# Tile 1's U dots in two halves of 64 tokens, half of its scatter under the dots, and a layer's end without its residual add and norm on VectorE

## What is computed

```
h = h + mixer(rmsnorm(h))             # layer 1: pooling; layer 0: attention and mLSTM
xn = rmsnorm(h, norm_ffn_g[layer])
expert, gate = product_key_top16(xn)  # 8 heads x 16 experts per token, of 16384
act = gelu(einsum('tkd,td->tk', u[expert], xn))
h = h + einsum('tk,tkd->td', gate * act, v[expert])

# pooling mixer of layer 1, hn = rmsnorm(h, norm_mix_g[1])
pooled = win_sum(hn) / count - hn     # windows 2/4/8/16 on four channel groups
h = h + einsum('sgc,gcd->sgd', pooled, pool_w) * layer_scale
```

## Time and profile before

| what | value |
|---|---|
| runs | 3057.61, 3053.96, 3052.4 us |
| median | 3053.96 us |
| profiled execution, its own time | 3056.03 us |
| its span | 3054.1 us |
| granted TensorE clock, mean | 0.864 |
| PE busy | 75% of the span |
| DVE busy | 71% |
| ACT busy | 22% |
| POOL busy | 37% |
| moved by DMA | 1059.10 MB, mean 347 GB/s |

### The profile page before, as it was taken

The page is one execution under the profiler, slowest core; times in us unless marked ns, Lnnn a source line. Parts: engine busy times, 40 slices in busy tenths (PEclk is TensorE's granted clock), DMA queues, the critical chain, the costliest instruction groups (busy, mean ns, idle before and its releaser), DMA issues.

```text
span 3054.1 us, 26189 instructions
## 1 busy us (share of the span) xinstructions
PE 2301.6 (75%) x9248; PEld 1683.1 (55%) x9248; DVE 2173.0 (71%) x3243; ACT 679.0 (22%) x1651; POOL 1136.6 (37%) x1028
## 2 busy tenths in 40 slices
PE   8999999688853410999999887888444019999996
PEld 4686555578753300666666556787433007666664
DVE  1342122899999999866666758999999988566667
ACT  1242120112229920300000011222399002000000
POOL 0000000423343333346666614333433333566664
PEclk9999999899985555999999988999755559999998
DMA  5333324899999999699999959999999996999998
GB/s 211 138 114 139 118 108 198 353 419 421 417 374 422 422 421 421 202 410 410 409 409 409 407 201 414 413 421 407 390 421 422 421 411 214 410 409 409 409 409 338
DMA packets 194530, 1059.10 MB, mean 347 GB/s; under 512 B 21856, under 2 KB 22240, under 8 KB 121312
## 3 DMA queue, kind: packets, MB, share of 16 engines
q0 software_dynamic: 147456, 805.37, 65.2%
q1 hardware_dynamic: 46944, 252.06, 20.8%
HBM read 1055.24 MB, written 2.10 MB: 346 GB/s over the span
## 4 chain that ended last, share of the span: by engine, by line
DMA 46%; PE 23%; DVE 23%; issue 3%; POOL 3%; ACT 1%; DVEq 0%; SPq 0%; ACTq 0%; POOLq 0%
DMA arena<-pu,idx_all 22%; DMA xnT<-pvg,idx_all 14%; DVE arena L1157 11%; DMA arena<-pvg,idx_all 10%; PE bank L1317 7%; DVE h L1183 3%; PE bank L1402 3%; PE bank L1623 2%; PE bank L1557 2%; PE bank L1631 2%; POOL xnT L470 1%; POOL arena L470 1%; PE low L1522 1%; PE bank L1591 1%; PE low L1511 1%
## 5 line engine op out<-in xcount | busy, mean ns | idle before, releaser
L1157 DVE CUSTOM_DVE_ANT_0 arena<-arena,low 128x2048 f32<-128x2048 f32 x420 | 952.6, 2286 | 71.7 <-DMA arena<-pu,idx_all 70.2
L455 POOL DMA_INDIRECT arena<-pu,idx_all x456 | 464.1, 1018 | 1358.8 <-DVE cst L1157 697.1
L1640 PE MATMUL low<-arena 128*128 128x512 f32 x2048 | 904.8, 601 | 9.4 <-DMA arena<-pvd 8.7
L1640 PEld LDWEIGHTS low<-arena 128*128 128x128 f32 x2048 | 597.2, 296 | 316.9 <-DMA arena<-pvd 71.8
L1183 DVE SCALAR_TENSOR_TENSOR h<-arena,cst,h 128x1024 f32<-128x1024 f32 x240 | 307.9, 1286 | 162.9 <-DMA arena<-pvg,idx_all 160.0
L1183 DVE SCALAR_TENSOR_TENSOR h<-xnT,cst,h 128x1024 f32<-128x1024 f32 x240 | 307.6, 1285 | 159.6 <-DMA xnT<-pvg,idx_all 157.1
L470 POOL DMA_INDIRECT arena<-pvg,idx_all x256 | 309.7, 1210 | 244.6 <-DVE h L1183 147.8
L470 POOL DMA_INDIRECT xnT<-pvg,idx_all x256 | 307.7, 1202 | 224.7 <-DVE h L1183 138.4
L1623 PE MATMUL bank<-arena 128*128 128x128 f32 x512 | 132.9, 441 | 201.6 <-ACT arena L747 201.6
L505 ACT ACTIVATE arena<-h 128x2048 f32<-128x2048 f32 (+1 forms) x10 | 17.4, 1740 | 1038.0 <-DVE h L1215 920.2
L1557 PE MATMUL bank<-xnT,arena 128*128 128x256 f32 (+1 forms) x1280 | 235.6, 347 | 11.1 <-issue 5.8
(11 more groups left out here) (233 smaller groups left out, 2203.2 us busy)
## 6 DMA issues: line engine op xcount, KB each, us to landing
arena<-pvd SPq DMA_DIRECT2D x256, 512.0 KB, 6.8
arena<-w_proj SPq DMA_DIRECT2D x22, 2048.0 KB, 7.6
arena<-wq SPq DMA_DIRECT2D x16, 2048.0 KB, 12.5
arena<-w_out SPq DMA_DIRECT2D x9, 2048.0 KB, 7.7
arena<-pu,idx_all POOLq DMA_INDIRECT x494, 14.8
gB<-gains SPq DMA_DIRECT2D x5, 1024.0 KB, 10.4
xnT<-pvg,idx_all POOLq DMA_INDIRECT x256, 14.0
arena<-pvg,idx_all POOLq DMA_INDIRECT x256, 13.9
```

The source lines that it names most:

```text
L455: nc.gpsimd.indirect_dma_start(U[t][slot], None, pu[L], bass.IndirectOffsetOnAxis(row(n), 0)).then_inc(u_got[t][slot], 16)
L1157: vec.tensor_tensor_reduce(out=u, in0=u, in1=low[:, :] if staged else xns[t], scale=1.0, scalar=0.0, op0=ALU.mult, op1=ALU.add, accum_out= ...
L1640: ins = mm(psum[2 * t + c][:, 0:VH], W[t][:, :, n], vdense[:, n % DR, c * VH:(c + 1) * VH], start=n == 0, stop=n == NK - 1)
```

## The change

It has four parts.

1. Tile 1's dots run in two halves of 64 tokens. A column of a half holds two expert slots: partitions 0 to 63 one, 64 to 127 the other, for the same 64 tokens. Indices and gates are rearranged to this layout by four small DMAs each. `duplicate` puts the half's tokens twice into PSUM with four matmuls by a selection matrix; the first dot of a half waits for it. The second half has a ring of six buffers, the last of which is the token tile itself.
2. The first half's weights are made after the 77th dot of tile 1 (index 76), and its 16 quads by ScalarE under the rest of the dots. VectorE makes the 16 quads of the second half after the last dot. `ND`, the number of diagonals, goes from 16 to 8. Two DMAs a half bring the weights back to the layout of the V adds.
3. `h` enters the dense sums by four matmuls with the identity; ScalarE copies the sums to `h` and squares them. The norm ahead of the pooling mixer is dropped: the rows of `PM` are scaled in place by VectorE, the gain is applied where the pooled banks leave PSUM. `pool_w` is loaded in two pieces, and `gain(2)` is not loaded.
4. Dense loads are paced by another rule.

```diff
-UT0, UT1, UP = 6, 7, 3
+UT0, UT1, UT2, UP = 6, 7, 6, 3
...
-LAST_T0 = 16
-ND, DG = 16, 2
+LAST_T0 = 8
+ND, DG = 8, 2
...
+HP = P // 2
+HQ = QUADS // 2
+NSEL = 2 * P + HP + 2
...
-        U = [ring(0, UT0), ring(W_AT + P * P, 2) + [fifth] + ring(0, 4)]
+        U = [ring(0, UT0), ring(W_AT + P * P, 2) + [fifth] + ring(0, 4), [fifth] + ring(0, 4) + [xn1]]
...
+        def pace(n):
+            return (NV - 3) * (n - 2) // NK - (NK - n) // 4
         def landed(m, ring):
...
             def load_vd(L, n):
-                if n > 8:
-                    sp.wait_ge(s["vacc_done"], L * NV + (NV - 8) * (n - 3) // NK)
+                if pace(n) > 0:
+                    sp.wait_ge(s["vacc_done"], L * NV + pace(n))
...
+                idx1 = idx_all[:, PH:2 * PH].rearrange("p g k -> p (g k)")
+                gates1 = gates[:, PH:2 * PH].rearrange("p g k -> p (g k)")
+                sp.dma_start(sel_all, selection).then_inc(s["ld_sel"], 16)
+                sp.wait_ge(s["idx_ready"], ROUTES * (L + 1))
+                for hf in range(2):
+                    for pp, pc, op, oc in quadrants(hf):
+                        sp.dma_start(idx_p[pp, pc], idx1[op, oc]).then_inc(s["ld_idx"], 16)
+                sp.wait_ge(s["gates_ready"], L + 1)
+                for hf in range(2):
+                    for pp, pc, op, oc in quadrants(hf):
+                        sp.dma_start(gates_p[pp, pc], gates1[op, oc]).then_inc(s["ld_gates"], 16)
+                def unfold(hf):
+                    sp.wait_ge(s["w_ready"], 3 * L + hf + 2)
+                    for b in range(2):
+                        sp.dma_start(wv[hf * HP:(hf + 1) * HP, 1, b * HP:(b + 1) * HP],
+                                     w_p[b * HP:(b + 1) * HP, hf, b * HP:(b + 1) * HP]).then_inc(s["ld_wv"], 16)
+                unfold(0)
                 for n in range(NK):
                     load_vd(L, n)
+                    if n == DR - 1:
+                        unfold(1)
...
-                        gain(2 + 2 * L)
+                        gain(3 + L)
                 if L == 0:
...
+                    sp.dma_start(gT, pool_gain).then_inc(s["ld_pm"], 16)
...
-                    sp.dma_start(poolw, pool_w.rearrange("p (g k c) -> p g k c", g=4, k=4)).then_inc(s["ld_pool"], 16)
+                    sp.dma_start(poolw[:, 0].rearrange("p k c -> p (k c)"), pool_w[:, 0:D]).then_inc(s["ld_pool0"], 16)
...
+                    sp.dma_start(poolw[:, 1:4].rearrange("p g k c -> p (g k c)"), pool_w[:, D:4 * D]).then_inc(s["ld_pool1"], 16)
...
-                    gain(3)
...
+                if t and d >= HP:
+                    d -= HP
+                    base = L * NDOT + ND0
+                    if d >= UT2:
+                        pool.wait_ge(s["dot_done"], base + HP + d - UT2 + 1)
+                    elif d == UT2 - 1:
+                        pool.wait_ge(s["dup_ready"], 2 * L + 2)
+                    else:
+                        pool.wait_ge(s["dot_done"], base + max(i for i in range(HP) if i % UT1 == d + 2) + 1)
+                    nc.gpsimd.indirect_dma_start(
+                        U[2][d % UT2], None, pu[L], bass.IndirectOffsetOnAxis(idx_p[:, HP + d:HP + d + 1], 0)
+                    ).then_inc(u_got[2][d % UT2], 16)
+                    return
...
+                    pool.wait_ge(s["ld_idx"], 64 * (L + 1))
...
-                    U[t][slot], None, pu[L], bass.IndirectOffsetOnAxis(row(n), 0)).then_inc(u_got[t][slot], 16)
+                    U[t][slot], None, pu[L], bass.IndirectOffsetOnAxis(idx_p[:, d:d + 1] if t else row(n), 0)
+                ).then_inc(u_got[t][slot], 16)
             def gather_v(L, m):
...
+                e.wait_ge(s["vacc_done"], NV * (o // 2) - LAST_T0 * (1 - t))
+                activation(xns[0][:, t * VG:(t + 1) * VG], h[:, t, VD:D], ACT.Square, accum_out=ss[:, t:t + 1]).then_inc(s["sq_done"], 1)
+            def add_dense(o, t):
+                e.wait_ge(s["dense_done"], o // 2)
+                for c in range(2):
+                    activation(h[:, t, c * VH:(c + 1) * VH], psum[2 * t + c][:, 0:VH], ACT.Copy).then_inc(s["acc_evac"], 1)
+                e.wait_ge(s["acc_evac"], NO * (o // 2 - 1) + 2 * t + 2)
...
+            def gelu(L):
+                e.wait_ge(s["dot_done"], L * NDOT + ND0)
+                e.wait_ge(s["picked"], (L + 1) * NUX)
+                activation(wv[:, 0], act[:, 0], ACT.Gelu).then_inc(s["gelu_done"], 1)
+            def gelu_half(L, hf):
+                e.wait_ge(s["dot_done"], L * NDOT + ND0 + (hf + 1) * HP)
+                cols = act[:, 1, hf * HP:(hf + 1) * HP]
+                activation(cols, cols, ACT.Gelu).then_inc(s["gelu_done"], 1)
...
+                e.wait_ge(s["st_mm"], 3 * L + hf + 2)
+                if hf == 0:
+                    activation(sT[:, 0:2], psum[6][:, 0:2 * P].rearrange("p (a b) -> p a b", a=2), ACT.Copy)
+                activation(sT[:, 2, hf * HP:(hf + 1) * HP], psum[6][:, 2 * P:2 * P + HP], ACT.Copy).then_inc(s["st_ready"], 1)
+            def one_hots(L, n):
+                b, q = n % 2, n % QUADS
...
             for L in range(LAYERS):
                 if L:
+                    e.wait_ge(s["ld_pm"], 32)
...
+                gelu(L)
+                turned(L)
...
-                gelu(L, 1)
-                turned(L, 1)
-                for q in range(QUADS):
-                    if q % (QUADS // ND) == 0:
-                        diagonal(L, q // (QUADS // ND))
-                    spread_out(L, 1, q)
-                norm(2 + 2 * L, 0)
-                square_dense(2 + 2 * L)
-                norm(2 + 2 * L, 1)
+                gelu_half(L, 0)
+                turned_half(L, 0)
+                for q in range(HQ):
+                    one_hots(L, QUADS + q)
+                    if q:
+                        spread_out(L, 1, q - 1)
+                spread_out(L, 1, HQ - 1)
+                gelu_half(L, 1)
+                turned_half(L, 1)
+                for q in range(HQ):
+                    if q % (HQ // ND) == 0:
+                        diagonal(L, q // (HQ // ND))
+                    spread_out(L, 1, HQ + q)
+                o = 2 + 2 * L
+                activation(root_load[:, 1 + L:2 + L], one, ACT.Sqrt)
+                add_dense(o, 0)
+                square_gathered(o, 0)
+                norm(o, 0)
+                add_dense(o, 1)
+                square_gathered(o, 1)
+                norm(o, 1)
...
             def link(ins):
...
-            def norm(o, t):
+            def mean_square(o, t):
...
-                if t and o in (2, 4):
-                    ins = vec.scalar_tensor_tensor(ms[:, tt], ss[:, tt], 1.0 / D, ms_half, ALU.mult, ALU.add)
+                if o in (2, 4):
+                    v.wait_ge(s["sq_dense"], TB * (o // 2 - 1) + t + 1)
+                    link(vec.tensor_scalar(ms_dense[:, tt], ss_dense[:, tt], 1.0 / D, EPS, ALU.mult, ALU.add))
+                    ins = vec.scalar_tensor_tensor(ms[:, tt], ss[:, tt], 1.0 / D, ms_dense[:, tt], ALU.mult, ALU.add)
...
+            def scale_pooling(t):
+                v.wait_ge(s["root_done"], TB * 2 + t + 1)
+                link(vec.reciprocal(rs[:, t:t + 1], rt[:, t:t + 1]))
+                if t == 0:
+                    v.wait_ge(s["ld_pm"], 32)
+                rows = PM[:, :, t, BAND[t]:S]
+                vec.tensor_scalar(rows, rows, rs[:, t:t + 1], None, ALU.mult).then_inc(s["xn_ready"], 1)
+            def norm(o, t):
+                tt = slice(t, t + 1)
+                if o in (0, 1, 3):
+                    mean_square(o, t)
...
-                v.wait_ge(s["ld_gain"], 16 * (o + 1))
+                v.wait_ge(s["ld_gain"], 16 * (o if o > 2 else o + 1))
...
-                d = dots.index(n) - ND0 * t
-                ring_ = UT1 if t else UT0
-                per_layer = [len(range(i, NDOT - ND0 if t else ND0, ring_)) for i in range(ring_)]
-                v.wait_ge(u_got[t][d % ring_], 16 * (L * per_layer[d % ring_] + d // ring_ + 1))
-                u = U[t][d % ring_]
-                staged = hk >= (2 if t else PK)
...
+                size = len(U[x])
+                v.wait_ge(u_got[x][d % size], 16 * (u_landed(L, x, d % size) + d // size + 1))
+                u = U[x][d % size]
+                staged = t or hk >= PK
+                if t and d == 0:
+                    v.wait_ge(s["dup_ready"], 2 * L + x)
+                elif t == 0 and hk == PK:
+                    v.wait_ge(s["xp_ready"], 4 * L + 4)
+                vec.tensor_tensor_reduce(out=u, in0=u, in1=low[:, :] if staged else xns[0], scale=1.0, scalar=0.0, op0=ALU.mult, op1=ALU.add,
...
+                    ins = vec.scalar_tensor_tensor(w_p[:, hf, b * HP:(b + 1) * HP], act[:, 1, cols], of_half[:, b:b + 1],
+                                                   gates_p[:, cols], ALU.mult, ALU.mult)
+                ins.then_inc(s["w_ready"], 1)
             def add_v(L, j):
...
+                if t and gathered[m - 1][0] == 0 and hk == 0:
```

(103 more changed lines are left out.)

140 lines of the change are left out of this document (80 added, 60 removed).

## The result

The changed kernel takes 3032.44 us (median; 3030.79 to 3032.51), the kernel before 3054.51 in the same runs (3052.4 to 3057.61): a ratio of 0.9925, 95% interval 0.9913 to 0.9938, 22.1 us less. The profiled execution has a span of 3030.7 us and a mean granted clock of 0.865. A difference to its 3032.44 us is taken across sets, so one of under 4 us is not told from nothing by the medians, and rests on the traces.

The account below looks back on a forecast made before the run. DMA was taken as the bound in tile 1's dots and the V stage, idle between. Savings of 36.6 less 10.9 and 1 gave 24.7 us off: 3031.3 profiled, 3029 against 3053.96 median; 8-in-10 range 3014 to 3047.

Parts of the forecast that it names:

- Bound and price: Whole kernel: what DMA bounds gets shorter only where DMA idles, so each part is priced in idle DMA time.
- part 1: Scatter after tile 1's last dot: 16 quads moved under the dots save 28.9 us, 18.3 of it idle DMA, per layer.
- Part 2, first wait: End of tile 0's dots: VectorE waits 3.7 us for four matmuls (bounds 3.6 and 7.2), own price near nothing.
- Part 2, second wait: After tile 1's 64th dot: VectorE stands 12.5 us in layer 0, some 14 in the second layer.
- the rival that counts the stands whole: Tile 1's halves: VectorE's waits count in full, 34 of 36.6 us, giving 3052 us, no change; chance 0.10.
- Part 2, what the DMA loses: Wait between the halves: DMA runs dry, last dot 5 us late, second layer 5.9; sum 10.9 us, bounds 9 and 19.
- 58 more at 2.486 us: Second half's dots after the wait: 58 further gathers at 2.486 us each, putting the last dot at 1229.2.
- dots more than 2.5 us apart: Dots after the gap behind tile 1's 64th dot: spacing above 2.5 us would make part 2 wrong.
- Index transfers: Before tile 1's first gather: first two gathers 1 to 5 us late, mostly made up; 1 us taken in all.
- Part 3: Layer ends after the V stage: stop before the last three adds, shorter norms; nothing within 4 us in each layer.
- The tail rival: Layer ends: matrix load and ACT chain each 4 to 6 us late, adding 8 to 12, 3039 us; chance 0.12.
- Dense as the bound: V stage's dense rows: clock falling to 1.2 GHz makes rows exceed their period, 3120 us, slower; chance 0.06.

Follow-up runs that it names:

- Experiment 1: Changed kernel with none of tile 1's quads under the dots: all 32 behind the last dot, 16 diagonals; 3069.07 us, ratio 1.0049.
- experiment 3: Changed kernel with the second duplication moved from ahead of tile 0's quad 28 to ahead of quad 26; 3019.46 us, ratio 0.989.
- experiment 4: Changed kernel with the gain tile as a seventh buffer in the second half's ring; 3028.65 us, ratio 0.9919.
- experiment 6: Changed kernel with four more index transfers ahead of the four, tile 1's first gather waiting for all eight; 3030.5 us, ratio 0.9927.
- experiment 7: experiment 3's kernel with the index transfers doubled from four to eight; 3024.45 us, ratio 0.9901.
- experiment 2: Kernel before with only the identity matmuls, ScalarE's copies and squares, the scaled pooling matrix and its loads; 3051.43 us, ratio 0.9992.
- experiment 10: Changed kernel with the second duplication ahead of quad 26 and dense loads released eight adds earlier, six buffers; 3015.91 us, ratio 0.9871.
- experiment 11: experiment 10's kernel with unread matmuls: two ahead of the first duplication, three ahead of each of tile 0's quads 22 to 25; 3016.47 us.

## Why the prediction was right, and where its sizes were off

- **Bound and price.** Each part priced in idle DMA time: shown. Experiment 1 gives 36.6 us for part 1 and the prediction had 36.6; by the traces it is 18.3 and 17.9 us. Of the scatter 28.9 us were to go; 29 (the 37.7 less 3.4 for the identity matmuls, against 63.4) to 30 were measured. ScalarE's last quad of the first half is copied at 1192.8 (computed: 1191), under the dots.
- **Part 2, first wait.** 3.7 us were taken, at full clock; it was 5.66 in both layers, within the bounds. Its effect on the dots was put near nothing, and is 1.3 and 0.8 us with the index transfers' in it.
- **Part 2, second wait.** 12.5 and 14 us were computed, 12.35 and 13.19 measured; restart 1077.1 computed, 1077.99 measured. The 14 is a slip: with the 64th dot of layer 1 at 2345.99 in the kernel before, the prediction's own count gives 12.9, and its 5.9 us for that layer fit this. The four waits add up to 36.9 us, and the two dot stages got 18.3 longer: the rival that counts the stands whole is out.
- **Part 2, what the DMA loses. This is the mis-sized term.** 10.9 us in both layers were taken, 7.4 + 8.8 = 16.2 measured, near the upper bound of 19. The step that failed is not the restart. The DMA was computed to run dry at 1074.6 and had its last landing at 1075.7; the first gather behind the wait was given 5.5 us, the shortest of the earlier trace rows, and took 6.3 and 5.5. Between the last landing before the stand and the first behind it lie 8.7 and 8.0 us, 6.2 and 5.5 more than one transfer needs; 5.5 had been computed for layer 0. What was too small is the rest, "58 more at 2.486 us": behind the restart the gathers landed every 2.516 and 2.531 us, which makes 1.8 and 2.6 us. That is 4.4 of the 5.3 us that are missing, and 0.8 is the longer landing in layer 0. The prediction had named dots more than 2.5 us apart as a sign against part 2; the sign came, if by little. The slower pace doesn't come from the dry stretch: experiment 3 has none and lands every 2.525 and 2.535 us, and all halved kernels whose landings the trace has lie from 2.51 to 2.54, those without halves at 2.49 to 2.50. A seventh buffer doesn't change it (2.52 and 2.53, experiment 4). Its cause stays open.
- **Index transfers.** 1 us was taken. The first gather was 3.0 us late (1 to 5 computed). The wait for TensorE does catch part of it, as the prediction says; it doesn't name the stand, which hides what is late in the first half (experiment 6). Their price by itself stays an estimate (experiment 7).
- **Part 3.** Nothing within 4 was taken, and alone it gave 2.3 us (experiment 2). Its mechanism came, smaller: the stop before the last three adds lasted 3.45 us where 5 to 7 were named. The tail rival needed 8 to 12 us more at that place. The prediction compared 36.3 us from the last gather to the end of the projections with 36.2 before; by the landings it is 31.1 with 31.8 before. It had read the gathers as in at 1755.9, from the GB/s of a window, and the last one landed at 1757.8. In layer 1 it is 14.4 us from the last landing to the end, 15.5 before, where 16 and 18 were named. The comparison held, and its two sides were both too long.
- **Dense as the bound** did not come: from 1650 to 1700 TensorE was busy 44 of 50 us at clock 1.00. The clock was 0.79 from 1715 to 1720 and 0.87 from 1720 to 1725, around a wait of 2.27 us for a dense row, and was back at 1.00 from 1725. By the rule that the prediction cites (the Trainium skill, TensorE: Matmul & The Clock Gate, section HAM oscillation) waits for DMA would have brought such falls again and again; the trace shows one of some 10 us in layer 0's dense stage and two in layer 1's.
- **The sum.** Forecast -24.7 us, measured -22.1. The medians of experiments 1 and 2 add up to -36.6 + 17.6 - 2.3 = -21.3, but this is no check, since each is the difference from one kernel to the next. The traces give one. From the last dot to the last add the changed kernel is 35.3 us shorter in both layers together; from the end of tile 0's dots to the end of tile 1's 18.3 longer, where 11.9 were taken; at the two ends 3.6 shorter, where nothing was taken; and 2.8 shorter in stages that the change hardly touches. So the profiled execution's 3032.5 us for a forecast of 3031.3 owes something to luck: 6.4 us of loss that the forecast lacked were met by 3.6 that it had put at nothing and 2.8 from stages that it had no reason to count.

## What to carry to other kernels

Where a stream of transfers is the bound, price a wait by how long it leaves the stream dry: the stand minus what the free buffers still hold, plus the landing of the first transfer behind it. The queue is empty then, and the shortest landing of the trace was a fair price (5.5 us, for 6.3 and 5.5). Be more careful with the pace behind it: 1.2 to 1.8% on 58 transfers made the larger error. And read landings from the transfers' own times, not from a window's GB/s. Ask what ends the wait. Here it was an engine's order, set by another engine, and moving four matmuls two quads forward gave 12 to 13 us, more than half of what the whole change had given. And before paying for a stop's removal near a stage's end, count from the last landing how long the stop holds up the end: here 3 to 4 us a layer, and not the 7 that seemed to be there.

## What the runs showed of the hardware

The same eight matmuls took from 3.67 to 6.74 us at the first duplication, from one execution to the next. Windows of the changed kernel over the first duplication, then of experiment 10's kernel:

```profile
905.00:907.00 2.00, 1.92 (x3) 0.97 (x4) 0.00 (x0) 0.00 (x0) 1.39 (x3) 0.64 0.88 291
907.00:909.00 2.00, 2.00 (x4) 0.68 (x3) 0.00 (x0) 0.00 (x0) 1.70 (x2) 0.51 1.00 385
```

```profile
905.00:907.00 2.00, 2.00 (x6) 0.95 (x5) 0.00 (x0) 0.00 (x0) 1.39 (x3) 1.00 1.00 389
907.00:909.00 2.00, 0.74 (x2) 0.00 (x0) 1.11 (x1) 0.00 (x0) 0.57 (x1) 1.00 0.98 381
```

TensorE had been busy at 1.00 and then idle for 2.08 us in the first, 2.67 in the second. The longer gap kept the clock, the shorter one lost it while TensorE was already working again. Over the 20 layers without fillers the clock stayed at 1.00 in seven, with gaps of 1.80 to 3.14 us, and fell in thirteen, with gaps of 1.96 to 3.43. So a gap before a burst can cost the burst its clock, and its length alone doesn't say whether it will. After gaps of 4.93 and 4.86 us (experiment 11, the second duplication) it was lost.

Small transfers in a loaded queue were dear. Issue to landing of the four index transfers of layer 0 (line 425, 885 to 893 us):

```profile
DMA to landing us min/median/max: 4.0/4.3/4.5
```

From the issue of the first to the gather that waits for all four it was 7.0 us; with eight, 11.9 us in experiment 6 (889.47 to 901.34) and 9.9 in experiment 7. In the two windows from 895 to 905 the DMA moved 183 and 112 GB/s in experiment 6, and 257 and 285 in the changed kernel. The Trainium skill, DMA: Bandwidth & Descriptors, section Anatomy of one DMA, gives a transfer a fixed cost of about 2 us whatever its size; the section is on transfers that GpSimd issues, and SyncE issues these. The trace doesn't agree with 2 us for four issued back to back at 0.6 us each while gathers fill the queues: the last, issued at 890.63, landed at 894.97, 4.3 us later.
